# Two products of the first MLP matrix in one 512-column matmul

## The chip, the cores and the metric

One core of a Trainium2 chip runs the whole program. It has a matrix engine (TensorE, PE in the rows, with its weight loads shown apart as PEld), a vector engine (VectorE, DVE), a scalar engine (ScalarE, ACT), GpSimd (POOL) and a sync engine (SP) that issues most of the transfers. The metric is the device time of one execution in microseconds; 1785.32 us is the median of three runs of the kernel before.

## The reference

A hybrid network on 256 tokens of width 1024 in float32: a first block (Fourier and gated delta-rule mixing, a convolutional feed-forward part), then two layers of a second kind. Each of these two layers ends in a plain MLP, which is the part that is changed:

```python
h = rms_norm(x, g_pre_mlp) * (1.0 + sc_f) + sh_f
f = jnp.square(jax.nn.relu(h @ w1)) @ w2
return x + gt_f * rms_norm(f, g_post_mlp)
```

`w1` is 1024 x 4096, `w2` 4096 x 1024; `h` has 256 rows.

## The kernel before

**Split products.** Float32 products are made of three products of a shorter type, `f32r` (`fp32r` in the rows). Each operand is split in a high part (a rounded copy) and a low part (what the copy left), and `mm3` (lines 341 to 344) adds high x high, high x low and low x high in one PSUM region. For a weight tile of 128 x 128 this is three matmuls of 256 columns with the weights `w_hi`, `w_hi`, `w_lo`: line 342 `w_hi` with `act_hi`, line 343 `w_hi` again with `act_lo`, line 344 `w_lo` with `act_hi`. Each matmul has a weight load of its own. In this text the three together are a unit.

**Chunks.** Weights come as chunks of 128 x 2048 values (1 MB, sixteen weight tiles), numbered `n` in the order of use. The sync engine loads chunk `n` in one of four slots `raw` as soon as chunk `n - 4` is done (`chunk_done`). ScalarE copies it to `w_hi` (`prep`, line 1071), VectorE subtracts and writes `w_lo` (`prep`, line 1607). `w_hi` and `w_lo` have two buffers each, so the two copies of chunk `n + 2` can begin only when chunk `n` is done, and have to be ready when chunk `n + 1` is done: `begin` makes TensorE wait for `lo_ready` before a chunk.

**The MLP.** It runs in two halves (`hf` 0 and 1) of 2048 hidden features. Each half has eight chunks of the first product (`feat_chunk`, or `mod_chunk` for the very first, which follows the modulated activations as they come), each 16 units into one bank of PSUM, 0 or 1 in turn, with its two output tiles side by side. Then come eight chunks of the second product (`deep_chunk`), in banks 2 to 5, which use `mlp_hi` and `mlp_lo`, the split of the squared hidden values.

Behind each first-product chunk stands a chain over two engines: ScalarE reads the bank through a ReLU into `relu` (line 1082, signals `evicted`), VectorE squares it into `rsq` (line 2334), ScalarE copies that to `mlp_hi` (line 1572), VectorE writes `mlp_lo` (line 2337). The order on each engine is written out by hand: ScalarE does `prep` of chunk `n + 2` first, then the chain of chunk `n`; VectorE likewise. After the last chunk of a half (`c` = 7) the chain comes first, and then `prep_halves` splits the weights of the second deep chunk, in two pieces of 1024 columns on each engine (lines 1077 and 1078, 1613 and 1615). The first deep chunk needs the last chain only in its last two units; the second deep chunk needs both pieces.

Of the kernel before, what the change touches and what calls it, by code (L numbers as in the profile page):

```python
# [90 lines left out]
def build_program(nc, io, layers=LAYERS):  # L91
# [6 lines left out]
    with ctx:  # L98
# [26 lines left out]
        act_hi = [at(f"act_hi{i}", [P, KT, T], F[i], f32r) for i in range(2)]  # L125
        act_lo = [at(f"act_lo{i}", [P, KT, T], F[2 + i], f32r) for i in range(2)]
# [153 lines left out]

        def JL(o):
            return o if o <= L_LRU else o - 1
# [15 lines left out]
        def _(sp):  # L298
            sp.dma_start(vec[:, :], io["vecs"]).then_inc(S("vec_loaded"), 16)
            sp.dma_start(cc[:, :], io["consts_common"]).then_inc(S("cc_loaded"), 16)  # L300
# [37 lines left out]
        def _(pe):  # L338
# [41 lines left out]
            def mod_chunk(wp, bank, s, m):  # L380

                for k in range(KT):
                    pe.wait_ge(S("mod_lo"), 8 * m + k + 1)
                    for b in range(2):
                        o = (b * KT + k) * P
                        last = mm3(ps[:, bank, b * T:(b + 1) * T], w_hi[:, wp, o:o + P], w_lo[:, wp, o:o + P],
                                   act_hi[s][:, k, :], act_lo[s][:, k, :], k + b == 0, k == KT - 1, shared=True)
                return last
# [106 lines left out]
            pe.wait_ge(S("cc_loaded"), 16)  # L495
# [382 lines left out]
            for L in range(layers):  # L878
# [153 lines left out]
                for hf in range(2):  # L1032
                    n = n0 + L_MLP + 16 * hf
                    j = j0 + JL(L_MLP) + 8 * hf
                    if hf == 0:
                        begin(n, j)
                        mod_chunk(n % 2, j % 2, 1, 4 + 2 * L).then_inc(S("chunk_done"), 1)
                        job(feat_chunk, n + 1, j + 1, 3, 1)
                        job(feat_chunk, n + 4, j + 4, 4, 1)
                    else:  # L1040
                        job(feat_chunk, n, j, 8, 1)
# [14 lines left out]
        def _(act):  # L1056
# [106 lines left out]
            act.wait_ge(S("eps_set"), 1)  # L1163
# [12 lines left out]
            for c in range(2):  # L1176
# [3 lines left out]
                if c == 0:  # L1180
                    act.wait_ge(S("pads"), 3)
# [183 lines left out]
            act.wait_ge(S("gpad_zero"), 1)  # L1365
# [31 lines left out]
            for L in range(layers):  # L1397
                n0, j0 = N_LAYER + L * LAYER_CH, J_LAYER + L * LAYER_J
                ns, sp_ = 5 + 4 * L, 4 * L
                if L == 0:  # L1400
                    act.dma_start(cu[:, 0:N_CB], io["consts_b"]).then_inc(S("consts_b"), 16)
# [161 lines left out]
                for hf in range(2):  # L1563
# [34 lines left out]
        def _(dve):  # L1598
# [115 lines left out]
            nc.vector.memset(eps[:, :], EPS).then_inc(S("eps_set"), 1)  # L1714
# [6 lines left out]
            dve.wait_ge(S("cc_loaded"), 16)  # L1721
# [16 lines left out]
            nc.vector.memset(pre_kv[:, :, :, 0:T + 2:T + 1], 0.0).then_inc(S("pads"), 1)  # L1738
            nc.vector.memset(pre_q[:, :, 0:1], 0.0).then_inc(S("pads"), 1)
            nc.vector.memset(pre_q[:, :, T + 1:T + 2], 0.0).then_inc(S("pads"), 1)  # L1740
# [253 lines left out]
            nc.vector.memset(gpad[:, :, :, :], 0.0).then_inc(S("gpad_zero"), 1)  # L1994
# [91 lines left out]
            for L in range(layers):  # L2086
# [42 lines left out]
                def cum():  # L2129
# [3 lines left out]
                    dve.wait_ge(S("consts_b"), 16)  # L2133
# [192 lines left out]
                for hf in range(2):  # L2326
# [3 lines left out]
                    def mlp_steps(i, c, j=j, hf=hf):  # L2330
                        s = (j + c) % 2
                        e = 8 * (2 * L + hf) + i + c
                        dve.wait_ge(S("evicted"), i + (j + c + 1))
                        tt(rsq[:, s, :], relu[:, s, :], relu[:, s, :], ALU.mult).then_inc(S("mlp_sq"), 1)  # L2334
                        dve.wait_ge(S("mlp_hi"), e + 1)
                        b = bass.ds((i + c) * 2, 2)
                        tt(mlp_lo[:, b, :], rsq[:, s, :].rearrange("p (b t) -> p b t", b=2), mlp_hi[:, b, :].bitcast(f32),
                           ALU.subtract).then_inc(S("mlp_ready"), 1)
                    job(n, 4, hook=mlp_steps)
                    for c in range(4, 7):  # L2340
                        prep(n + c + 2, (n + c + 2) % RAW, (n + c) % 2)
                        mlp_steps(0, c)
                    mlp_steps(0, 7)
# [147 lines left out]
```

## Time and profile before

| what | value |
|---|---|
| median of three runs | 1785.32 us (1782.82 to 1785.48) |
| profiled execution, its span | 1786.7 us, no other time of it is given |
| TensorE matmuls, busy | 1704.3 us, 95% of the span, 15394 |
| TensorE weight loads, busy | 1606.0 us, 90% |
| VectorE, busy | 1097.3 us, 61% |
| ScalarE, busy | 813.0 us, 46% |
| DMA, mean over the span | 184 GB/s |
| mean granted clock of TensorE | 0.988 |

A matmul's length in the rows is the time from its start to the end of its last result; matmuls overlap, so the pace is read from one start to the next. The first products of the MLP run from about 995 to 1041 us and 1087 to 1128 us in the first layer, and from about 1593 to 1639 and 1685 to 1726 us in the second; the second products fill the 40 to 46 us behind each.

### The profile page before, as it was taken

The page shows a single profiled execution, that of the slowest core. Times are in us where ns is not written, and L with a number is a line of the kernel's source. Part 1 is how long each engine was busy: PE and PEld are TensorE (multiplying, and loading weights), DVE is VectorE, ACT ScalarE, POOL GpSimd, SP SyncE. Part 2 cuts the span into 40 slices and gives each one's busy share as a digit, 9 for nine tenths or more (in the row PEclk, how much of TensorE's full clock was granted, in tenths as well). Part 3 has the DMA queues.
Part 4 walks back from the last instruction along what each step waited for, and adds up shares of the span by engine and source line. Part 5 has one row for each costly group of instructions (what it writes and reads, how often), then busy time and mean ns, then how long its engine had stood idle before and what let it go on. Part 6 is the DMA issues. An engine that isn't in the chain of part 4 may idle for free.

```text
span 1786.7 us, 34649 instructions
## 1 busy us (share of the span) xinstructions
PE 1704.3 (95%) x15394; PEld 1606.0 (90%) x15394; DVE 1097.3 (61%) x1367; ACT 813.0 (46%) x1051; POOL 34.2 (2%) x68
## 2 busy tenths in 40 slices
PE   5998899999999899999999999999999999999997
PEld 4896788799988899999999899979999999979997
DVE  3476664679853565468775755555447778666463
ACT  3245414433333535447654444435454575445352
POOL 0000000000000000000000000000000000000000
PEclk8998999999999999999999999999999999999999
DMA  9676433654568444445555355525444445535552
GB/s 397 254 279 235 183 147 128 235 191 167 201 224 328 173 164 162 139 149 178 177 189 182 117 191 196 189 98 186 142 142 165 165 166 189 189 110 185 200 189 71
DMA packets 45210, 329.32 MB, mean 184 GB/s; under 512 B 5008, under 2 KB 5008, under 8 KB 5392
## 3 DMA queue, kind: packets, MB, share of 16 engines
q1 hardware_dynamic: 35712, 258.63, 41.8%
q0 software_dynamic: 9216, 67.11, 9.8%
q8 instruction: 114, 1.87, 0.4%
q10 hardware_dynamic: 144, 1.51, 0.2%
q14 instruction: 24, 0.20, 0.0%
HBM read 326.18 MB, written 1.05 MB: 183 GB/s over the span
## 4 chain that ended last, share of the span: by engine, by line
PE 81%; DVE 9%; ACT 6%; DMA 2%; issue 1%; POOL 0%; SPq 0%; ACTq 0%; DVEq 0%; POOLq 0%
PE ps L342 20%; PE ps L344 20%; PE ps L343 20%; PE ps L395 4%; DVE w_lo L1607 3%; PE ps L467 3%; ACT w_hi L1071 3%; PE ps L446 3%; DMA ada_raw<-ada 2%; PE ps L630 1%; PE ps L641 1%; DVE rstd L1654 1%; DVE x L1692 1%; PE ps L973 1%; DVE rsq L2334 1%
## 5 line engine op out<-in xcount | busy, mean ns | idle before, releaser
L1607 DVE TENSOR_TENSOR w_lo<-raw,w_hi 128x2048 fp32r<-128x2048 f32 x207 | 474.5, 2292 | 489.4 <-ACT w_hi L1071 489.0
L342 PE MATMUL ps<-act_hi,w_hi 128*128 128x256 f32 x2672 | 756.6, 283 | 15.0 <-DVE act_lo L1676 4.6
L343 PE MATMUL ps<-act_lo,w_hi 128*128 128x256 f32 x2672 | 744.9, 279 | 0.0
L344 PE MATMUL ps<-act_hi,w_lo 128*128 128x256 f32 x2672 | 744.8, 279 | 0.0
L1071 ACT ACTIVATE w_hi<-raw 128x2048 fp32r<-128x2048 f32 (+1 forms) x229 | 421.7, 1842 | 551.5 <-PE ps L344 549.0
L342 PEld LDWEIGHTS ps<-act_hi,w_hi 128*128 128x128 f32 x2672 | 504.1, 189 | 25.3 <-issue 16.3
L343 PEld LDWEIGHTS ps<-act_lo,w_hi 128*128 128x128 f32 x2672 | 505.4, 189 | 1.1 <-issue 0.2
L344 PEld LDWEIGHTS ps<-act_hi,w_lo 128*128 128x128 f32 x2672 | 503.6, 188 | 0.0
L342 PE MATMUL ps<-mlp_hi,w_hi 128*128 128x256 f32 x512 | 143.0, 279 | 0.2
L343 PE MATMUL ps<-mlp_lo,w_hi 128*128 128x256 f32 x512 | 141.5, 276 | 0.0
L344 PE MATMUL ps<-mlp_hi,w_lo 128*128 128x256 f32 x512 | 141.5, 276 | 0.0
L342 PEld LDWEIGHTS ps<-mlp_hi,w_hi 128*128 128x128 f32 x512 | 96.1, 188 | 0.8 <-DVE w_lo L1615 0.6
L2031 DVE SCALAR_TENSOR_TENSOR gacc<-gpad,vectors,gacc 128x256 f32<-128x256 f32 x176 | 84.6, 481 | 19.7 <-ACT gacc L1344 14.3
L343 PEld LDWEIGHTS ps<-mlp_lo,w_hi 128*128 128x128 f32 x512 | 96.3, 188 | 0.2
L344 PEld LDWEIGHTS ps<-mlp_hi,w_lo 128*128 128x128 f32 x512 | 96.1, 188 | 0.0
L395 PE MATMUL ps<-h_up,raw 128*128 128x256 f32 x352 | 82.4, 386 | 1.9 <-ACT h_up L1334 1.6
L395 PEld LDWEIGHTS ps<-h_up,raw 128*128 128x128 f32 x352 | 65.4, 192 | 13.5 <-ACT h_up L1334 2.9
L342 PE MATMUL ps<-w_hi,act_hi 128*128 128x256 f32 x256 | 72.2, 282 | 0.0
L467 PE MATMUL ps<-ada_raw,silu_c_wide 128*32 128x256 f32 x1024 | 64.7, 392 | 7.7 <-DMA ada_raw<-ada 7.6
L344 PE MATMUL ps<-w_hi,act_lo 128*128 128x256 f32 x256 | 71.4, 279 | 0.0
L343 PE MATMUL ps<-w_lo,act_hi 128*128 128x256 f32 x256 | 71.3, 278 | 0.0
L467 PEld LDWEIGHTS ps<-ada_raw,silu_c_wide 128*32 128x32 f32 x1024 | 30.2, 111 | 31.5 <-DMA ada_raw<-ada 10.3
(407 smaller groups left out, 2053.3 us busy)
## 6 DMA issues: line engine op xcount, KB each, us to landing
raw<-stream SPq DMA_DIRECT2D x233, 1024.0 KB, 4.9
ada_raw<-ada POOLq DMA_DIRECT2D x64, 1024.0 KB, 7.0
ada_f<-ada SPq DMA_DIRECT2D x4, 1024.0 KB, 14.9
ada_a<-ada SPq DMA_DIRECT2D x3, 1024.0 KB, 20.6
consts_stage<-consts_a SPq DMA_DIRECT2D x1, 1728.0 KB, 32.7
consts_stage<-consts_b ACTq DMA_DIRECT2D x1, 1472.0 KB, 10.6
x<-xT SPq DMA_DIRECT2D x1, 1024.0 KB, 7.9
xc<-ctxT SPq DMA_DIRECT2D x1, 1024.0 KB, 9.9
```

Of the source, the lines that this page charges most:

```text
L342: mm(out, ah, bh, start=first, stop=False, skip_group_check=shared)
L343: mm(out, ah, bl, start=False, stop=False, skip_group_check=shared)
L344: return mm(out, al, bh, start=False, stop=last, skip_group_check=shared)
L395: mm(ps[:, bank, 0:T], raw[:, slot, k * P:(k + 1) * P], h_up[:, k, :], start=k == 0, stop=k == KT - 1)
L446: last = mm(ps[:, 7, 0:T], omean, sq[:, b, :], start=b == 0, stop=b == KT - 1)
L467: last = mm(ps[strip:strip + 32, bank, c * T:(c + 1) * T], cs_wide[:, k, 32 - 3 * j:64 - 3 * j], ada_raw[:, c, k * T:(k + 1) * T], start=j ...
L630: last = mm(ps[r:r + 64, INV_BANK[q], j * 64:(j + 1) * 64], B01[d][r:r + 64, t0 + j // 4, j % 4, r:r + 64], Tm[r:r + 64, q, j, :], start=T ...
L641: last = mm(ps[r:r + 64, INV_BANK[q], j * 32:(j + 1) * 32], Uc[r:r + 64, q, j, :], half(X[r:r + 64, q, j, :], d, 1 << lvl), start=True, st ...
L973: last = mm(out, s1[:, h * 2 + m, t * P:(t + 1) * P], vtok_r[:, m, h * T:(h + 1) * T], start=m == 0, stop=m == t)
L1071: act_(w_hi[:, s2, o:CH], raw[:, s4, o:CH], ACT.Copy).then_inc(S("hi_ready"), 1)
L1607: tt(w_lo[:, s2, :], raw[:, s4, :], w_hi[:, s2, :].bitcast(f32), ALU.subtract).then_inc(S("lo_ready"), 1)
L2031: ins = stt(acc, src, w, acc, ALU.mult, ALU.add)
```

## The change

The activations' high and low parts are put in one tensor, `act_both`, so that `act_hi` and `act_lo` of the same tile can be read by one matmul as 2 x 256 columns. In the first MLP product a unit becomes two matmuls: `w_hi` with 512 columns (high and low activations side by side) into a whole bank, and `w_lo` with `act_hi` added onto the first 256 columns of that bank. A chunk now fills two banks instead of one, (0, 1) or (6, 7) in turn.

The two halves of a bank are added when it is read: ScalarE copies the right halves of both banks to `relu` (signal `side_out`), VectorE adds the left halves (signal `evicted`), and then squares with the ReLU in the same instruction, max with 0 and multiply. On ScalarE the copy of the bank moves ahead of `prep`; on VectorE the add and the square stand ahead of `prep`, and `mlp_lo` behind it. Some semaphores are merged under one name (`cleared`, `consts_loaded`), with counts raised to match; one such line stands in the diff.

```diff
@@ place of the activations @@
-        act_hi = [at(f"act_hi{i}", [P, KT, T], F[i], f32r) for i in range(2)]
-        act_lo = [at(f"act_lo{i}", [P, KT, T], F[2 + i], f32r) for i in range(2)]
+        act_both = at("act_both", [P, 2, 2, KT, T], F[0], f32r)
+        act_hi = [act_both[:, 0, i, :, :] for i in range(2)]
+        act_lo = [act_both[:, 1, i, :, :] for i in range(2)]
...
+        MLP_BANKS = ((0, 1), (6, 7))
...
-            sp.dma_start(cc[:, :], io["consts_common"]).then_inc(S("cc_loaded"), 16)
+            sp.dma_start(cc[:, :], io["consts_common"]).then_inc(S("consts_loaded"), 16)
...
@@ TensorE: new functions @@
+            def wide(banks, wp, s, b, k):
+
+                o = (b * KT + k) * P
+                mm(ps[:, banks[b], :], w_hi[:, wp, o:o + P], act_both[:, :, s, k, :], start=k == 0, stop=False, skip_group_check=True)
+                return mm(ps[:, banks[b], 0:T], w_lo[:, wp, o:o + P], act_hi[s][:, k, :], start=False, stop=k == KT - 1,
+                          skip_group_check=True)
+
+            def wide_chunk(wp, bank, s):
+
+                for b in range(2):
+                    for k in range(KT):
+                        last = wide(MLP_BANKS[bank], wp, s, b, k)
+                return last
+
+            def wide_mod_chunk(wp, bank, s, m):
+
+                for k in range(KT):
+                    pe.wait_ge(S("mod_lo"), 8 * m + k + 1)
+                    for b in range(2):
+                        last = wide(MLP_BANKS[bank], wp, s, b, k)
                 return last
...
@@ TensorE: the MLP @@
-                        mod_chunk(n % 2, j % 2, 1, 4 + 2 * L).then_inc(S("chunk_done"), 1)
-                        job(feat_chunk, n + 1, j + 1, 3, 1)
-                        job(feat_chunk, n + 4, j + 4, 4, 1)
+                        wide_mod_chunk(n % 2, j % 2, 1, 4 + 2 * L).then_inc(S("chunk_done"), 1)
+                        job(wide_chunk, n + 1, j + 1, 3, 1)
+                        job(wide_chunk, n + 4, j + 4, 4, 1)
                     else:
-                        job(feat_chunk, n, j, 8, 1)
+                        job(wide_chunk, n, j, 8, 1)
...
@@ ScalarE: the MLP @@
-                        evict(relu[:, s, :], s, i + (n + c), ACT.Relu)
+                        bank = MLP_BANKS[s][0]
+                        act.wait_ge(S("chunk_done"), n + c + 1)
+                        act_(relu[:, s, :].rearrange("p (b t) -> p b t", b=2), ps[:, bank:bank + 2, T:2 * T], ACT.Copy)\
+                            .then_inc(S("side_out"), 1)
+                        if c < 7:
+                            prep(n + c + 2, (n + c + 2) % RAW, (n + c) % 2)
                         act.wait_ge(S("mlp_sq"), e + 1)
                         act_(mlp_hi[:, bass.ds((i + c) * 2, 2), :], rsq[:, s, :].rearrange("p (b t) -> p b t", b=2), ACT.Copy)\
                             .then_inc(S("mlp_hi"), 1)
-                    job(n, j, 4, None, hook=mlp_steps)
-                    for c in range(4, 7):
-                        prep(n + c + 2, (n + c + 2) % RAW, (n + c) % 2)
+                    for c in range(8):
                         mlp_steps(0, c)
-                    mlp_steps(0, 7)
                     prep_halves(n + 9)
...
@@ VectorE: the MLP @@
-                    def mlp_steps(i, c, j=j, hf=hf):
-                        s = (j + c) % 2
-                        e = 8 * (2 * L + hf) + i + c
-                        dve.wait_ge(S("evicted"), i + (j + c + 1))
-                        tt(rsq[:, s, :], relu[:, s, :], relu[:, s, :], ALU.mult).then_inc(S("mlp_sq"), 1)
-                        dve.wait_ge(S("mlp_hi"), e + 1)
-                        b = bass.ds((i + c) * 2, 2)
+                    def mlp_square(c, n=n, j=j, hf=hf):
+                        s, bank = (j + c) % 2, MLP_BANKS[(j + c) % 2][0]
+                        dve.wait_ge(S("side_out"), 8 * (2 * L + hf) + c + 1)
+                        y = relu[:, s, :].rearrange("p (b t) -> p b t", b=2)
+                        tt(y, ps[:, bank:bank + 2, 0:T], y, ALU.add).then_inc(S("evicted"), 1)
+                        dve.wait_ge(S("evicted"), j + c + 1)
+                        stt(rsq[:, s, :], relu[:, s, :], 0.0, relu[:, s, :], ALU.max, ALU.mult).then_inc(S("mlp_sq"), 1)
+
+                    def mlp_low(c, j=j, hf=hf):
+                        s, b = (j + c) % 2, slice(2 * c, 2 * c + 2)
+                        dve.wait_ge(S("mlp_hi"), 8 * (2 * L + hf) + c + 1)
                         tt(mlp_lo[:, b, :], rsq[:, s, :].rearrange("p (b t) -> p b t", b=2), mlp_hi[:, b, :].bitcast(f32),
                            ALU.subtract).then_inc(S("mlp_ready"), 1)
-                    job(n, 4, hook=mlp_steps)
-                    for c in range(4, 7):
+                    for c in range(7):
+                        mlp_square(c)
                         prep(n + c + 2, (n + c + 2) % RAW, (n + c) % 2)
-                        mlp_steps(0, c)
-                    mlp_steps(0, 7)
+                        mlp_low(c)
+                    mlp_square(7)
+                    mlp_low(7)
                     prep_halves(n + 9, 2 * L + hf + 1)
                     job(n + 8, 8 if hf == 0 else 6)
```

On TensorE, at the end of the first product of a half, where the second product begins. Before, the last unit of the first product and the first of the second:

```order
L342 MATMUL ps<-act_hi_54,w_hi 128x256
L343 MATMUL ps<-act_lo_56,w_hi 128x256
L344 MATMUL ps<-act_hi_54,w_lo 128x256
L342 MATMUL ps<-mlp_hi,w_hi 128x256 [waits lo_ready,mlp_ready]
L343 MATMUL ps<-mlp_lo,w_hi 128x256
L344 MATMUL ps<-mlp_hi,w_lo 128x256
```

Now:

```order
L396 MATMUL ps<-act_both,w_hi 128x512
L397 MATMUL ps<-act_both,w_lo 128x256
L345 MATMUL ps<-mlp_hi,w_hi 128x256 [waits lo_ready,mlp_ready]
L346 MATMUL ps<-mlp_lo,w_hi 128x256
L347 MATMUL ps<-mlp_hi,w_lo 128x256
```

The three matmuls of a unit with their three weight loads have become two; the second product's are as they were.

On ScalarE, the last two chunks of a half (`c` = 6 and 7) and the halves of the second deep chunk's weights. Before:

```order
L1071 ACTIVATE w_hi<-raw 128x2048 [waits chunk_done,raw_loaded0]
L1082 ACTIVATE relu<-ps 128x512 [waits chunk_done]
L1572 ACTIVATE mlp_hi<-rsq 128x512 [waits mlp_sq]
L1082 ACTIVATE relu<-ps 128x512 [waits chunk_done]
L1572 ACTIVATE mlp_hi<-rsq 128x512 [waits mlp_sq]
L1077 ACTIVATE w_hi<-raw 128x1024 [waits chunk_done,raw_loaded1]
L1078 ACTIVATE w_hi<-raw 128x1024
```

Now:

```order
L1597 ACTIVATE relu<-ps 128x512 [waits chunk_done]
L1096 ACTIVATE w_hi<-raw 128x2048 [waits chunk_done,raw_loaded0]
L1602 ACTIVATE mlp_hi<-rsq 128x512 [waits mlp_sq]
L1597 ACTIVATE relu<-ps 128x512 [waits chunk_done]
L1602 ACTIVATE mlp_hi<-rsq 128x512 [waits mlp_sq]
L1102 ACTIVATE w_hi<-raw 128x1024 [waits chunk_done,raw_loaded1]
L1103 ACTIVATE w_hi<-raw 128x1024
```

The copy out of PSUM stands ahead of the weight copy for `c` = 6; for `c` = 7 and the halves the order is the same.

On VectorE, the same place. Before:

```order
L1607 TENSOR_TENSOR w_lo<-raw,w_hi 128x2048 [waits hi_ready]
L2334 TENSOR_TENSOR rsq<-relu 128x512 [waits evicted]
L2337 TENSOR_TENSOR mlp_lo<-rsq,mlp_hi 128x512 [waits mlp_hi]
L2334 TENSOR_TENSOR rsq<-relu 128x512 [waits evicted]
L2337 TENSOR_TENSOR mlp_lo<-rsq,mlp_hi 128x512 [waits mlp_hi]
L1613 TENSOR_TENSOR w_lo<-raw,w_hi 128x1024 [waits half_hi]
L1615 TENSOR_TENSOR w_lo<-raw,w_hi 128x1024 [waits hi_ready]
```

Now:

```order
L2361 TENSOR_TENSOR relu<-ps,relu 128x512 [waits side_out]
L2363 SCALAR_TENSOR_TENSOR rsq<-relu 128x512 [waits evicted]
L1634 TENSOR_TENSOR w_lo<-raw,w_hi 128x2048 [waits hi_ready]
L2368 TENSOR_TENSOR mlp_lo<-rsq,mlp_hi 128x512 [waits mlp_hi]
L2361 TENSOR_TENSOR relu<-ps,relu 128x512 [waits side_out]
L2363 SCALAR_TENSOR_TENSOR rsq<-relu 128x512 [waits evicted]
L2368 TENSOR_TENSOR mlp_lo<-rsq,mlp_hi 128x512 [waits mlp_hi]
L1640 TENSOR_TENSOR w_lo<-raw,w_hi 128x1024 [waits half_hi]
L1642 TENSOR_TENSOR w_lo<-raw,w_hi 128x1024 [waits hi_ready]
```

Each chunk has one instruction more, the add from PSUM; add and square have moved ahead of `w_lo`, and for `c` = 7 the add stands ahead of the square and so of the two pieces of `w_lo`.

## Rows read from the trace of the kernel before

**Rows 1.** The share of the chain that ended last, by engine (page, part 4).
```profile
PE 81%; DVE 9%; ACT 6%; DMA 2%; issue 1%; POOL 0%; SPq 0%; ACTq 0%; DVEq 0%; POOLq 0%
```

**Rows 2.** Busy time by stretch, first half: us, busy by engine in order, PEclk.
```profile
995.00:1041.00 46.00, 45.74 (x385) 45.68 (x386) 29.28 (x33) 23.99 (x27) 0.00 (x0) 1.00 0.47 161
```

**Rows 3.** Timeline, TensorE matmuls, first half of the MLP: start, length, line.
```profile
1009.83 0.28 PE L342 MATMUL ps<-act_hi,w_hi 128*128 128x256 f32 x1
...
1010.18 0.28 PE L342 MATMUL ps<-act_hi,w_hi 128*128 128x256 f32 x1
...
1011.95 0.28 PE L342 MATMUL ps<-act_hi,w_hi 128*128 128x256 f32 x1
```

**Rows 4.** Timeline, TensorE weight loads, the same stretch.
```profile
1010.07 0.19 PEld L342 LDWEIGHTS ps<-act_hi,w_hi 128*128 128x128 f32 x1
```

**Rows 5.** Timeline, TensorE matmuls, second half of the MLP.
```profile
1095.03 0.28 PE L343 MATMUL ps<-act_lo,w_hi 128*128 128x256 f32 x1
...
1097.07 0.28 PE L343 MATMUL ps<-act_lo,w_hi 128*128 128x256 f32 x1
```

**Rows 6.** Groups by shape, TensorE (first row 1095 to 1115 us): count, busy, mean.
```profile
L342 PE MATMUL ps<-act_hi,w_hi 128*128 128x256 f32 x60 | 16.6, 276 | 0.0
...
L973 PE MATMUL ps<-vtok_r,s 128*128 128x256 f32 x48 | 10.7, 379 | 0.0
...
L923 PE MATMUL ps<-s 128*128 128x128 f32 x32 | 6.2, 274 | 0.0
```

**Rows 7.** Timeline, TensorE, sixteen f32 matmuls of 256 columns in a row.
```profile
373.46 3.61 PE L395 MATMUL ps<-h_up,raw 128*128 128x256 f32 x16
```

**Rows 8.** Timeline, TensorE weight loads under matmuls of two columns.
```profile
35.91 1.86 PEld L511 LDWEIGHTS ps<-strip_rows,mod_rows 128*128 128x128 f32 x16 [0.41 <-issue]
```

**Rows 9.** Timeline, ScalarE: one steady chunk, the last chunk of each half.
```profile
1012.92 1.92 ACT L1071 ACTIVATE w_hi<-raw 128x2048 fp32r<-128x2048 f32 x1
1014.74 0.58 ACT L1082 ACTIVATE relu<-ps 128x512 f32<-128x512 f32 x1
...
1041.12 0.60 ACT L1082 ACTIVATE relu<-ps 128x512 f32<-128x512 f32 x1
...
1128.47 0.58 ACT L1082 ACTIVATE relu<-ps 128x512 f32<-128x512 f32 x1
```

**Rows 10.** Timeline, VectorE: one steady chunk, the last chunk of each half.
```profile
1014.87 2.29 DVE L1607 TENSOR_TENSOR w_lo<-raw,w_hi 128x2048 fp32r<-128x2048 f32 x1 [1.37 <-ACT w_hi L1071]
...
1041.76 0.69 DVE L2334 TENSOR_TENSOR rsq<-relu 128x512 f32<-128x512 f32 x1
...
1045.24 1.22 DVE L1615 TENSOR_TENSOR w_lo<-raw,w_hi 128x1024 fp32r<-128x1024 f32 x1
...
1129.21 0.68 DVE L2334 TENSOR_TENSOR rsq<-relu 128x512 f32<-128x512 f32 x1
```

**Rows 11.** Groups by shape, VectorE.
```profile
L1684 DVE TENSOR_TENSOR s<-ps,rstd 128x512 f32<-128x512 f32 x16 | 10.6, 685 | 0.1
...
L2292 DVE SCALAR_TENSOR_TENSOR act_lo<-s,act_hi 128x512 fp32r<-128x512 f32 x8 | 5.3, 686 | 1.7 <-ACT act_hi L1502 1.7
```

**Rows 12.** Timeline, TensorE: second deep chunk of each half; a stage of layer two.
```profile
1046.58 0.33 PE L342 MATMUL ps<-mlp_hi,w_hi 128*128 128x256 f32 x1
...
1133.96 0.38 PE L342 MATMUL ps<-mlp_hi,w_hi 128*128 128x256 f32 x1
1134.18 0.28 PE L343 MATMUL ps<-mlp_lo,w_hi 128*128 128x256 f32 x1
...
1136.22 0.28 PE L343 MATMUL ps<-mlp_lo,w_hi 128*128 128x256 f32 x1
...
1500.99 0.39 PE L342 MATMUL ps<-act_hi,w_hi 128*128 128x256 f32 x1 [0.61 <-DVE w_lo L1607]
1501.22 0.28 PE L343 MATMUL ps<-act_lo,w_hi 128*128 128x256 f32 x1
...
1503.57 0.28 PE L342 MATMUL ps<-act_hi,w_hi 128*128 128x256 f32 x1
```

More of the change, by code:

```diff
@@ L387, in mod_chunk @@
                                    act_hi[s][:, k, :], act_lo[s][:, k, :], k + b == 0, k == KT - 1, shared=True)
+                return last
[8 more added lines that the diff above has]
+                        last = wide(MLP_BANKS[bank], wp, s, b, k)
+                return last
+            def wide_mod_chunk(wp, bank, s, m):
[3 more added lines that the diff above has]
+                        last = wide(MLP_BANKS[bank], wp, s, b, k)
                 return last
@@ L492, in small_tr @@
                 return last
-            pe.wait_ge(S("cc_loaded"), 16)
+            pe.wait_ge(S("consts_loaded"), 16)
             norm(0, norm_sq1)
@@ L1162, in _ @@
             act_(cth[:, :], vec[:, 0:3 * KT], ACT.Tanh, scale=0.5).then_inc(S("c_tanh"), 1)
-            act.wait_ge(S("eps_set"), 1)
+            act.wait_ge(S("cleared"), 1)
             act.wait_ge(S("x_loaded"), 16)
@@ L1180, in _ @@
                 if c == 0:
-                    act.wait_ge(S("pads"), 3)
+                    act.wait_ge(S("cleared"), 4)
                 act_(pre_q[:, 2 * c:2 * c + 2, 1:T + 1], ps[:, n % 2, :].rearrange("p (b t) -> p b t", b=2), ACT.Copy)\
@@ L1364, in up_mid @@
                 act_(mid_hi1[:, bass.ds(i + (c - 2), 1), :], gm[:, c % 2:c % 2 + 1, :], ACT.Copy).then_inc(S("mid_hi"), 1)
-            act.wait_ge(S("gpad_zero"), 1)
+            act.wait_ge(S("cleared"), 5)
             for c in range(4):
@@ L1400, in _ @@
                 if L == 0:
-                    act.dma_start(cu[:, 0:N_CB], io["consts_b"]).then_inc(S("consts_b"), 16)
+                    act.dma_start(cu[:, 0:N_CB], io["consts_b"]).then_inc(S("consts_loaded"), 16)
                 norm_x(ns, x, a6, 5 + 8 * L)
@@ L1711, in softplus @@
                 order(stt(dst, e, 2.0, m, ALU.mult, ALU.add))
-            nc.vector.memset(eps[:, :], EPS).then_inc(S("eps_set"), 1)
+            nc.vector.memset(eps[:, :], EPS).then_inc(S("cleared"), 1)
             dve.wait_ge(S("c_tanh"), 1)
@@ L1720, in _ @@
             order(nc.vector.tensor_copy(cs_wide[:, :, 32:35], cs[:, :, :].rearrange("p a k -> p k a")))
-            dve.wait_ge(S("cc_loaded"), 16)
+            dve.wait_ge(S("consts_loaded"), 16)
             red(sel[:, :], ident.rearrange("p (s r) -> p r s", s=4), AX, ALU.add).then_inc(S("cs_ready"), 1)
@@ L1737, in _ @@
             prep(1, 1, 1)
-            nc.vector.memset(pre_kv[:, :, :, 0:T + 2:T + 1], 0.0).then_inc(S("pads"), 1)
-            nc.vector.memset(pre_q[:, :, 0:1], 0.0).then_inc(S("pads"), 1)
-            nc.vector.memset(pre_q[:, :, T + 1:T + 2], 0.0).then_inc(S("pads"), 1)
+            nc.vector.memset(pre_kv[:, :, :, 0:T + 2:T + 1], 0.0).then_inc(S("cleared"), 1)
+            nc.vector.memset(pre_q[:, :, 0:1], 0.0).then_inc(S("cleared"), 1)
+            nc.vector.memset(pre_q[:, :, T + 1:T + 2], 0.0).then_inc(S("cleared"), 1)
             job(N_Q, 1)
@@ L1993, in _ @@
                  lambda b: tt(act_lo[1][:, b, :], h_up[:, b, :], act_hi[1][:, b, :].bitcast(f32), ALU.subtract))
-            nc.vector.memset(gpad[:, :, :, :], 0.0).then_inc(S("gpad_zero"), 1)
+            nc.vector.memset(gpad[:, :, :, :], 0.0).then_inc(S("cleared"), 1)
             order(nc.vector.memset(sw_wide[:, :, 8:16], 0.0))
@@ L2132, in cum @@
                     dve.wait_ge(S("cum_ev"), L + 1)
-                    dve.wait_ge(S("consts_b"), 16)
+                    dve.wait_ge(S("consts_loaded"), 32)
                 def fox_scores(h0):
```

## The prediction

> **What bounds the kernel now.** I read the share of the last chain first: TensorE carries 81% of it [rows 1]. Then the stretch of the changed stage: in the first half of the MLP TensorE is busy 45.74 of 46 us, VectorE 29.28 and ScalarE 23.99, at a granted clock of 1.00, so the upper of the two levels, 2.4 GHz [rows 2]. The stage is TensorE's, and the question is what paces its matmuls. So, third, the timeline, from start to start: eighteen steps in the first half take 2.12 us, 117.8 ns each [rows 3]; eighteen steps of the same work in the second half 2.04 us, 113.3 ns [rows 5]. The same form thus has two paces, each kept for whole stages at an unchanged clock. The weight loads explain both: a load starts with the matmul before its own (1010.07) and its matmul starts 0.11 us later [rows 3, 4]; and sixteen matmuls of only two columns, where nothing but the load can set the pace, have their loads (1.86 - 0.19) / 15 = 111.3 ns apart [rows 8]. A 256-column matmul is over in the time that the next load needs. Fewer loads for the same columns is a real saving.
>
> **What a unit costs afterwards.** A unit of three matmuls takes 353 ns in the first half and 340 ns in the second. The 512-column `f32r` matmul is not in the trace. Its nearest relative is an `f32` matmul of half the columns: `f32` with 128 columns lasts 274 ns, `f32r` with 256 lasts 276 [rows 6], so `f32r` with 512 should behave as `f32` with 256, which lasts 379 ns [rows 6] and follows itself in (3.61 - 0.38) / 15 = 215.3 ns [rows 7]. That is longer than any load, so the load of `w_lo` hides completely. The 256 columns of `w_lo` then have to cover the load of the next `w_hi`, as now: between 111.3 ns (load alone) and 117.8 ns; I take the middle of the two paces, 115.5. New unit: 331 ns.
>
> First half of a layer: seven chunks of 16 units, 112 x (353 - 331) = 2.5 us. Second half: eight chunks, 128 x (340 - 331) = 1.15 us. The first chunk of a layer, which follows the modulated activations one by one, I count as nothing. Both layers: 7.2 us off. Ends: with 326.6 ns a unit, 9.3 us; with no saving at all (512 columns costing two old paces), 0. A loss I exclude: the columns streamed are the same and a load goes.
>
> **What is added in the middle of a half, and hides.** ScalarE's copy of two half banks has the size of the old ReLU read (0.58 us [rows 9]) but now stands ahead of the weight copy. The chain from a chunk's end to finished weights was w_hi start to w_lo start 1.95 us, then 2.29 us [rows 9, 10]; with 0.58 in front and about 0.06 us for the signal it is 4.9 us, against a new chunk of 16 x 331 = 5.3 us. VectorE's add out of PSUM (685 ns) and the square with max (686 ns for that form) [rows 11] stand ahead of `w_lo`, but run while ScalarE makes `w_hi` (1.92 us), so they cost nothing. Slack 0.4 us; were it gone, each overrun would be paid by TensorE at every chunk. A PSUM bank pair is free after the add, a whole chunk before it is written again. Renamed semaphores and the joined tensor move nothing.
>
> **What is added at the end of a half, and shows.** After the last chunk the chain stands ahead of the two weight pieces of the second deep chunk, on both engines. In the first half it now runs: read 1041.12, square 1041.76 [rows 9, 10], last piece of `w_lo` 1045.24 + 1.22 = 1046.46, and TensorE's second deep chunk starts at 1046.58 [rows 10, 12], a start that TensorE itself would have made at about the same time (its 48 matmuls at 117.8 ns fill 5.65 us). So the cover is just used up, and whatever lengthens the chain is paid in full. The change puts the add ahead of the square: 0.685 us and 0.04 us to the next instruction (the step from the read's end at 1041.72 to the square), 0.725 us. In the second half the square starts only at 1129.21, held by the chunk before; afterwards it would start at 1128.47 + 0.58 + 0.04 + 0.725 = 1129.81 [rows 9, 10], so 0.6 us later. The first deep chunk itself does not wait, since its last two units come some 4.8 us after its start. Per layer 1.33 us, both layers 2.7 us back. Ends: 0.4 us per half (a shorter add) and 1 us.
>
> **The pace after the longer wait.** TensorE keeps whichever of its two paces it falls into after a wait. Behind the 1133.96 start, delayed by the same `w_lo`, it runs eighteen steps in 2.04 us, 113.3 ns; behind a wait of 0.61 us for `w_lo` in layer two it runs twenty steps in 2.35 us, 117.5 ns [rows 12]. Now all four second products start their second chunk after a wait of 0.6 to 1 us. The slow pace would cost 48 x 4.5 ns = 0.216 us a chunk: seven chunks in a first half, and two in a second half, where norm matmuls then break the run: 1.5 and 0.4 us. I take half of the 3.9 us for both layers, 1.9 us, because the rows show one case of each kind. Ends 0 and 3.9.
>
> **Sum.** -7.2 + 2.7 + 1.9 = -2.6 us. Made in the profiled execution it takes its span from 1786.7 to 1784.1 us; the median of the runs lies 1.4 us under that span, so 1785.3 - 2.6 = 1782.7 us.
>
> **A rule against it.** The trace gives 113.3 and 117.8 ns for 256 columns and 215.3 ns for twice the streaming time [rows 3, 5, 7]. The Trainium skill, "TensorE: Matmul & The Clock Gate", section "Back-to-back issue gap", puts a lone warm gap at the columns over 2.4 GHz plus about 2.5 ns, 109.2 and 215.8 ns; the trace agrees with the second and not with the first. An estimate by that page would make a unit 327.5 ns before and 325.0 after, 1.2 us gained in 480 units, and the kernel 3.4 us slower. I go by the rows, which show the load; that the load is not what is saved is rival 2, priced by rows.
>
> **Rivals.**
> 1. The fast pace survives the waits in all four second products. For it: the shorter waits of now all led to it [rows 12]. Against: the wait at 1500.99. -7.2 + 2.7 = -4.5, 1780.8 us.
> 2. The load is not what is saved: the excess belongs to every matmul, so 512 columns cost an old pace plus the lengthening of 105 ns (379 - 274, rows 6), 222.8 or 218.3 ns, and the pair 340.6 or 331.6. Gain 224 x 12.7 + 256 x 8.4 ns = 5.0 us, sum -0.4, 1784.9 us: the change would then remove less than it says. For it: both paces lie above the load's 111.3 ns. Against: sixteen `f32` matmuls show no such excess [rows 7].
> 3. Slower: the second products fall into the slow pace in all 28 chunks behind the waits, norm breaks included. 28 x 0.216 = 6.0 us, sum +1.5, 1786.9 us. It turns the sign from 21 slow chunks on (4.5 / 0.216). For it: the whole first half of now runs slow [rows 3]; against: in the second half of now the fast pace is kept [rows 5].
>
> **Chances.** Forecast 0.50 (own range 1780.5 to 1785), rival 1 0.25, rival 2 0.13, rival 3 0.12. The stages of layer two's mixer start at other moments than now and may change pace too, some 2 us either way, which widens each case. Range 1776.5 to 1787: the low end is the 9.3 us gain with the fast pace (-6.6, 1778.7) and those 2 us, the high end is rival 3. About 3.6 us, 0.2%, is what a measurement of this kernel can tell from no change: faster by more 0.42 (most of rival 1, a third of the forecast, the mixer's part), within 0.50, slower 0.08.
>
> **What would show it.** Right: first products with starts 215 and 113 to 118 ns apart in turn, chunks of about 5.3 us without waits of TensorE for `w_lo`; at each half's end an add of 0.69 us ahead of the square and a wait of 0.6 to 1 us ahead of the second deep chunk. Wrong: a 512-column matmul paced above 225 ns; weight chains longer than a chunk; no wait at the second deep chunk, or one at the first, for `mlp_lo`.

## The result, and the profile after

The changed kernel takes 1793.11 us (median of 18 runs, 1789.45 to 1799.48) against 1784.06 us for the kernel before in the same series (18 runs). The ratio is 1.0048, 95% interval 1.0032 to 1.0064. (It is an estimate from the runs of both kernels and differs a little from the quotient of the two medians, 1.0051.) The changed kernel is slower, outside the range of the prediction, and on the other side from the forecast.

The chain that ended last (page, part 4), by engine, against 81% of TensorE [rows 1]:

```profile
PE 83%; DVE 8%; ACT 5%; DMA 2%; issue 1%; SPq 0%; DVEq 0%; ACTq 0%
```

The first half's stretch, busy time by engine, then granted clock, DMA share and GB/s (after):

```profile
989.00:1035.00 46.00, 45.84 (x258) 39.49 (x259) 34.70 (x41) 23.15 (x27) 0.00 (x0) 1.00 0.45 160
```

As in [rows 2], TensorE is full and at the upper level of its clock. A third of the loads is gone, VectorE has 5.4 us more, and no wait shows: the loss must lie in TensorE's own matmuls. Their starts in the first half and in the second (timeline, TensorE, after):

```profile
1009.74 0.40 PE L396 MATMUL ps<-act_both,w_hi 128*128 128x512 f32 x1
1009.97 0.28 PE L397 MATMUL ps<-act_both,w_lo 128*128 128x256 f32 x1
1010.09 0.40 PE L396 MATMUL ps<-act_both,w_hi 128*128 128x512 f32 x1
...
1012.57 0.40 PE L396 MATMUL ps<-act_both,w_hi 128*128 128x512 f32 x1
...
1096.71 0.40 PE L396 MATMUL ps<-act_both,w_hi 128*128 128x512 f32 x1
1096.94 0.28 PE L397 MATMUL ps<-act_both,w_lo 128*128 128x256 f32 x1
1097.06 0.40 PE L396 MATMUL ps<-act_both,w_hi 128*128 128x512 f32 x1
...
1099.18 0.40 PE L396 MATMUL ps<-act_both,w_hi 128*128 128x512 f32 x1
```

Eight units in 2.83 us and seven in 2.47 us are 353 ns a unit, in steps of 235 and 118 ns. That is three times 117.8, the unit of [rows 3] to the nanosecond: a 512-column matmul costs two 256-column ones at their slow pace, and the load that is gone gives nothing back. In the second half, which ran at 113.3 before [rows 5], the unit has become 13 ns longer.

The chains on ScalarE and VectorE (timeline of each, after; steady chunk, then the last chunk of the first half):

```profile
1006.76 0.60 ACT L1597 ACTIVATE relu<-ps 128x512 f32<-128x512 f32 x1 [2.73 <-PE ps L397]
1007.25 1.91 ACT L1096 ACTIVATE w_hi<-raw 128x2048 fp32r<-128x2048 f32 x1
...
1035.03 0.60 ACT L1597 ACTIVATE relu<-ps 128x512 f32<-128x512 f32 x1 [2.73 <-PE ps L397]
```

```profile
1007.39 0.69 DVE L2361 TENSOR_TENSOR relu<-ps,relu 128x512 f32<-128x512 f32 x1 [0.95 <-ACT relu L1597]
1008.11 0.69 DVE L2363 SCALAR_TENSOR_TENSOR rsq<-relu 128x512 f32<-128x512 f32 x1
1009.19 2.29 DVE L1634 TENSOR_TENSOR w_lo<-raw,w_hi 128x2048 fp32r<-128x2048 f32 x1 [0.39 <-ACT w_hi L1096]
...
1035.66 0.69 DVE L2361 TENSOR_TENSOR relu<-ps,relu 128x512 f32<-128x512 f32 x1 [0.95 <-ACT relu L1597]
1036.38 0.69 DVE L2363 SCALAR_TENSOR_TENSOR rsq<-relu 128x512 f32<-128x512 f32 x1
...
1039.86 1.22 DVE L1642 TENSOR_TENSOR w_lo<-raw,w_hi 128x1024 fp32r<-128x1024 f32 x1
```

In the steady chunk the weights are finished at 1009.19 + 2.29 = 1011.48, 4.7 us after the read of the bank began (4.9 predicted), inside a chunk of 5.65 us; VectorE even waits 0.39 us for `w_hi`. At the half's end the add runs from 1035.66 and the square follows at 1036.38, 0.72 us later than the add began [compare rows 9, 10]. The second deep chunk of each half (timeline, TensorE, after):

```profile
1040.36 0.28 PE L347 MATMUL ps<-mlp_hi,w_lo 128*128 128x256 f32 x1
1041.13 0.39 PE L345 MATMUL ps<-mlp_hi,w_hi 128*128 128x256 f32 x1 [0.49 <-DVE w_lo L1642]
1041.36 0.28 PE L346 MATMUL ps<-mlp_lo,w_hi 128*128 128x256 f32 x1
...
1043.47 0.28 PE L346 MATMUL ps<-mlp_lo,w_hi 128*128 128x256 f32 x1
...
1132.34 0.39 PE L345 MATMUL ps<-mlp_hi,w_hi 128*128 128x256 f32 x1 [0.50 <-DVE w_lo L1642]
1132.57 0.28 PE L346 MATMUL ps<-mlp_lo,w_hi 128*128 128x256 f32 x1
...
1134.62 0.28 PE L346 MATMUL ps<-mlp_lo,w_hi 128*128 128x256 f32 x1
```

TensorE now waits 1041.13 - 1040.36 - 0.12 = 0.65 us, as predicted. Behind the wait of the first half eighteen steps take 2.11 us (117 ns), behind that of the second 2.05 us (114 ns). In [rows 12] both went on at the quick pace.

Stage by stage, from the differences of matmul starts in the traces (from the last of the matmuls that only keep TensorE busy ahead of the MLP to the first deep one, and so on, at last to the first matmul behind the last deep one; both layers alike within 0.02 us):

| us per layer | first product, half 0 | deep, half 0 | first product, half 1 | deep, half 1 | whole MLP |
|---|---|---|---|---|---|
| before | 46.97 | 43.79 | 43.52 | 47.40 | 181.68 |
| after | 46.97 | 45.98 | 45.22 | 48.00 | 186.18 |
| difference | 0.00 | +2.19 | +1.70 | +0.60 | +4.50 |

Two layers make +9.0 us, the size of the difference between the medians. The profiled spans differ by only 0.9 us (1787.6 and 1786.7): in that one execution of the changed kernel the parts ahead of the two MLPs, where the change alters no work, happened to take 6.1 and 2.0 us less. The span of one profile would have passed the change as neutral.

### The profile page after: what moved, and what is told of

It reads as the page before. It is cut to its first block, busy times and chain, and to the rows that moved or that the text cites. A ratio compares the mean times of both kernels' runs of the same rounds, so it can differ in the third digit from the quotient of the medians.

```text
span 1787.6 us, 33657 instructions
## 1 busy us (share of the span) xinstructions
PE 1704.4 (95%) x14882; PEld 1582.5 (89%) x14882; DVE 1119.4 (63%) x1399; ACT 811.3 (45%) x1051; POOL 34.1 (2%) x68
## 4 chain that ended last, share of the span: by engine, by line
PE 83%; DVE 8%; ACT 5%; DMA 2%; issue 1%; SPq 0%; DVEq 0%; ACTq 0%
PE ps L345 18%; PE ps L346 18%; PE ps L347 18%; PE ps L396 7%; PE ps L420 4%; PE ps L397 3%; PE ps L492 3%; PE ps L471 2%; DVE w_lo L1634 2%; DMA raw<-stream 1%; ACT w_hi L1096 1%; PE ps L655 1%; DVE rstd L1681 1%; PE ps L666 1%; DMA ada_raw<-ada 1%
## 5 line engine op out<-in xcount | busy, mean ns | idle before, releaser
L345 PE MATMUL ps<-act_both,w_hi 128*128 128x256 f32 x2160 | 612.4, 284 | 14.9 <-DVE act_both L1703 5.3
L346 PE MATMUL ps<-act_both,w_hi 128*128 128x256 f32 x2160 | 601.8, 279 | 0.0
L347 PE MATMUL ps<-act_both,w_lo 128*128 128x256 f32 x2160 | 601.6, 279 | 0.0
L345 PEld LDWEIGHTS ps<-act_both,w_hi 128*128 128x128 f32 x2160 | 407.6, 189 | 23.6 <-issue 13.9
L346 PEld LDWEIGHTS ps<-act_both,w_hi 128*128 128x128 f32 x2160 | 408.7, 189 | 1.1 <-issue 0.2
L347 PEld LDWEIGHTS ps<-act_both,w_lo 128*128 128x128 f32 x2160 | 407.3, 189 | 0.0
L396 PE MATMUL ps<-act_both,w_hi 128*128 128x512 f32 x512 | 182.0, 399 | 1.4 <-DVE act_both L1698 1.4
L397 PE MATMUL ps<-act_both,w_lo 128*128 128x256 f32 x512 | 143.9, 281 | 0.0
L396 PEld LDWEIGHTS ps<-act_both,w_hi 128*128 128x128 f32 x512 | 96.2, 188 | 27.4 <-issue 3.0
L397 PEld LDWEIGHTS ps<-act_both,w_lo 128*128 128x128 f32 x512 | 96.1, 188 | 0.0
L345 PE MATMUL ps<-w_hi,act_both 128*128 128x256 f32 x256 | 72.1, 282 | 0.0
```

The source lines that it names most:

```text
L345: mm(out, ah, bh, start=first, stop=False, skip_group_check=shared)
L346: mm(out, ah, bl, start=False, stop=False, skip_group_check=shared)
L347: return mm(out, al, bh, start=False, stop=last, skip_group_check=shared)
L396: mm(ps[:, banks[b], :], w_hi[:, wp, o:o + P], act_both[:, :, s, k, :], start=k == 0, stop=False, skip_group_check=True)
L397: return mm(ps[:, banks[b], 0:T], w_lo[:, wp, o:o + P], act_hi[s][:, k, :], start=False, stop=k == KT - 1, skip_group_check=True)
```

## The experiments

The theory formed from these traces: fetching different columns of `f32r` paces these matmuls, at 0.443 or 0.460 ns a column (113.3 and 117.8 over 256), the weight load runs beside it, and a joined matmul saves nothing. The expectations call it theory C, and call the two paces levels: quick (113.3) and slow (117.8). Its rival, from the prediction: loads pace the narrow matmuls, and something in the wide form (two pieces of 256 columns, or a new wait) takes the saving back.

**The wide matmul alone taken back.** Everything of the change stays, the 512 columns are issued as two matmuls.

```diff
-                mm(ps[:, banks[b], :], w_hi[:, wp, o:o + P], act_both[:, :, s, k, :], start=k == 0, stop=False, skip_group_check=True)
+                mm(ps[:, banks[b], 0:T], w_hi[:, wp, o:o + P], act_hi[s][:, k, :], start=k == 0, stop=False, skip_group_check=True)
+                mm(ps[:, banks[b], T:2 * T], w_hi[:, wp, o:o + P], act_lo[s][:, k, :], start=False, stop=False, skip_group_check=True)
```

> The changed kernel with each 512-column matmul split again into two of 256 columns, into the left and right half of the same bank; banks, chain and add stay as changed. Theory C (the pace of an f32r matmul goes by its columns, at 0.443 or 0.460 ns a column, whatever its weight loads; the level is kept until TensorE waits): three starts 118 ns apart where the pair took 235 + 118, a unit again 353 ns, a layer's MLP 186 us, the whole within 2 us of the changed kernel's 1793 us. Theory W (the wide matmul is slow by itself and brings the loss): only the longer chain is left, 1784 + 2.7 = about 1787 us.

1787.08 us, ratio to before 1.0005 (0.9983 to 1.0026). With the same chains, banks and adds, but narrow matmuls, the kernel can't be told from the kernel before. So the joining itself brought the larger part of the loss; the longer chain's 2.7 us lie inside this interval. Theory C, which expected 353 ns here too and about 1793 us, is not borne out: the number of columns alone does not set the time of a unit. The trace (timeline, TensorE):

```profile
1011.87 0.28 PE L397 MATMUL ps<-act_both,w_hi 128*128 128x256 f32 x1
...
1014.13 0.28 PE L396 MATMUL ps<-act_both,w_hi 128*128 128x256 f32 x1
...
1051.39 0.39 PE L345 MATMUL ps<-mlp_hi,w_hi 128*128 128x256 f32 x1 [0.71 <-DVE w_lo L1643]
```

Twenty steps in 2.26 us: 113 ns, in all four first products and, up to the norm matmuls, all four second ones. The stages are 45.41, 44.53, 43.52 and 47.99 us, 181.45 in all. The wait behind the longer chain is there (0.71). Its price in the second half is 47.99 - 47.40 = 0.59 us. In the first half 44.53 - 43.79 = 0.74 us mixes in a pace, since the first deep chunk before still ran at 117.8; against the second trace of the kernel before (below), where it ran at 113.3, the price is 44.53 - 43.91 = 0.62 us.

The profiled execution took 1795.46 us, one of the longest of the twelve, although all these stages ran at the quick pace: the rest of the program varies too.

**A quarter of the load.** The kernel before with 32 of 128 weight columns in the chunks of the first product behind the modulated one.

```diff
...
+                        last = mm3(ps[0:32, bank, b * T:(b + 1) * T], w_hi[:, wp, o:o + 32], w_lo[:, wp, o:o + 32],
+                                   act_hi[s][:, k, :], act_lo[s][:, k, :], k == 0, k == KT - 1)
...
```

> The kernel before, first products with 32 of the 128 weight columns (the other 96 output rows are left out): a quarter of the weight load under the same 256 streamed columns. Theory C: starts stay 113 or 118 ns apart, 15 first-product chunks a layer as long as before. If the load paces 256 columns: starts come down to about 108 ns (half of the 215.3 ns of f32 with 256 columns), 5.2 us a chunk.

Its matmuls, and its loads (timeline of each):

```profile
1011.02 0.28 PE L344 MATMUL ps<-act_hi,w_lo 128*32 128x256 f32 x1
...
1013.29 0.28 PE L343 MATMUL ps<-act_lo,w_hi 128*32 128x256 f32 x1
```

```profile
1011.02 0.11 PEld L342 LDWEIGHTS ps<-act_hi,w_hi 128*32 128x32 f32 x1
```

A load lasts 0.11 us instead of 0.19 [rows 4], and twenty matmuls take 2.27 us, still 113 ns, in all four first products. So the load does not pace them: its being the limit was the prediction's main step, and that falls here. A single run, 1787.82 us.

**The same column over and over, narrow and wide.** Here the loads are whole, but a matmul reads one activation column over and over (the wide one a column of the high part, then one of the low part); first the kernel before, then the changed one.

```diff
...
+                                   act_hi[s][:, k, 0:1].to_broadcast([P, T]), act_lo[s][:, k, 0:1].to_broadcast([P, T]),
...
```

```diff
+                cols = act_both[:, :, s, k, 0:1].to_broadcast([P, 2, T]) if same else act_both[:, :, s, k, :]
+                hi = act_hi[s][:, k, 0:1].to_broadcast([P, T]) if same else act_hi[s][:, k, :]
...
```

> The kernel before, first products (but the first chunk of a layer) with the same single column of the activations read 256 times (step 0), so the products are not the reference's. If fetching 256 different columns of four bytes each sets the 113 and 118 ns: starts come down to 108 ns, half of the 215.3 ns of f32. If the array or the write to PSUM sets it: 113 or 118 ns as before.

> The changed kernel with the same single column of the high and of the low activations read 256 times each (step 0) in the first products, but for the first chunk of a layer, so the products are not the reference's. Theory F (fetching different columns sets the pace above the load's 112 ns; the load saved is real but lies under it): with no columns to fetch the pair shows the saving, 215 + 112 = 327 ns against 3 x 112 = 335 of the same trial with three matmuls. If the wide matmul is slow for another reason: 235 + 112 or more.

Narrow, then wide (timeline, TensorE, of each):

```profile
1002.83 0.28 PE L343 MATMUL ps<-act_lo,w_hi 128*128 128x256 f32 x1
...
1005.06 0.28 PE L342 MATMUL ps<-act_hi,w_hi 128*128 128x256 f32 x1
```

```profile
1014.85 0.38 PE L398 MATMUL ps<-act_both,w_hi 128*128 128x512 f32 x1
1015.07 0.27 PE L399 MATMUL ps<-act_both,w_lo 128*128 128x256 f32 x1
1015.17 0.38 PE L398 MATMUL ps<-act_both,w_hi 128*128 128x512 f32 x1
...
1017.79 0.38 PE L398 MATMUL ps<-act_both,w_hi 128*128 128x512 f32 x1
```

Narrow: twenty steps in 2.23 us, 111.5 ns, neither of the two values expected but that of the loads alone (111.3 [rows 8]). Wide: nine units in 2.94 us, 327 ns, in steps of 218 and 109, as expected. So a saving like the one that the prediction counted exists, 3 x 111.5 - 327 = 7.5 ns a unit where it counted 9 to 22, but only where one column is repeated. This run writes whole banks too, so the width of the result is not what holds the wide form at 235 ns. With real columns a narrow matmul needs 113.3 ns even with the short load above, so the load of 111 ns is already covered. Whether it is the fetching of new columns or their changing values that takes the remainder, these two runs do not tell apart. A single run of each: 1775.92 and 1787.87 us.

**Is it the two pieces?** The 512 columns are read as one contiguous piece of `act_both` (other products than the reference's).

```diff
+                cols = act_both[:, 0, s, min(k, 6):min(k, 6) + 2, :] if one else act_both[:, :, s, k, :]
+                mm(ps[:, banks[b], :], w_hi[:, wp, o:o + P], cols, start=k == 0, stop=False, skip_group_check=True)
...
```

> The changed kernel with the 512 columns read as one piece (high parts of two neighbouring tiles, so the right halves hold other sums than the reference's), not as two pieces 16 KB apart; the first chunk of a layer as changed. If the two pieces hold the wide matmul at its slow level: pairs of 227 + 113 = 340 ns. If not: 235 + 118 = 353 ns again.

235 and 118 ns as before, first products 46.96 and 45.22 us: not the two pieces. A single run, 1792.27 us.

**Only 512-column matmuls.** The second matmul of a unit gets 512 columns too.

```diff
-                return mm(ps[:, banks[b], 0:T], w_lo[:, wp, o:o + P], act_hi[s][:, k, :], start=False, stop=k == KT - 1,
+                return mm(ps[:, banks[b], :], w_lo[:, wp, o:o + P], act_both[:, :, s, k, :], start=False, stop=k == KT - 1,
...
```

> The changed kernel with 512 columns for w_lo too (low weights times low activations is added to the sum, which makes it a little more exact). Theory C: time goes by columns, so a pair costs 471 ns at 0.460 ns a column or 453 at 0.443, and a first-product chunk 7.5 or 7.25 us. If only a matmul of 512 columns followed by one of 256 is held at the slow level: 453. If a 512-column matmul had the 215 ns of two f32 passes and the 20 ns were a price of the pair: 431.

Steps of 233 ns in the first half, and in the second of 236 ns (`w_lo`) and 230 to 231 ns (`w_hi`) in turn, 467 ns a pair in both: 0.45 to 0.46 ns a column, not the 0.42 (215.3 / 512) that the prediction assumed. So a 512-column matmul is not slow only for having a narrow one behind it. A single run, 1853.36 us.

**The wide form with a quarter of the load.**

```diff
+                mm(ps[0:32, banks[b], :], w_hi[:, wp, o:o + 32], act_both[:, :, s, k, :], start=k == 0, stop=False, skip_group_check=True)
+                return mm(ps[0:32, banks[b], 0:T], w_lo[:, wp, o:o + 32], act_hi[s][:, k, :], start=False, stop=k == KT - 1,
...
```

> The changed kernel with 32 of 128 weight columns in the first products (96 output rows left out): loads of 108 instead of 188 ns under 512 and 256 columns. If the full load that falls into a 512-column stream holds it at the slow level: 340 ns a pair. If the level has nothing to do with loads, as 113 ns with thin loads for 256 columns suggests: 353 ns.

The narrow step stays at 118 ns, so the slow pace does not need the long load either; the wide one is 224 in some places and 232 to 233 in others, 228 on average, against 235, so a unit takes 347 ns, neither of the two values expected. In this one trace the load thus has a small part in the wide form's slow pace, and not the whole. A single run, 1790.08 us. Why the wide form falls to the slow pace is not settled by this.

**The wait at the second deep chunk taken away, without and with the change.** The two weight pieces are split around the copy to `mlp_hi` (and `mlp_lo`): the first now stands ahead of it, the second behind.

```diff
+            def prep_halves(n, between):
...
                 act_(w_hi[:, n % 2, 0:CH // 2], raw[:, n % RAW, 0:CH // 2], ACT.Copy).then_inc(S("half_hi"), 1)
+                between()
                 act_(w_hi[:, n % 2, CH // 2:CH], raw[:, n % RAW, CH // 2:CH], ACT.Copy).then_inc(S("hi_ready"), 1)
...
```

> The kernel before, with the first half of the second deep chunk's weights made ahead of mlp_hi and mlp_lo of the last chunk, on both engines, so that TensorE has no wait at the second deep chunk. If the level is kept until TensorE waits (theory C): the second products and the next first products stay at the slow 117.8 ns of the first half, deep products of the first half 45.3 instead of 43.8 us, first products of the second half 45.2 instead of 43.5 us, the waits of 0.04 and 0.4 us gone: some 2.8 us a layer, 1784 + 5.6 = about 1790 us, although a wait was removed. If waits only cost what they last: 1784 - 0.9 = about 1783 us.

> The changed kernel with the same reordering at the end of a half. Theory C: the waits of 0.65 and 0.7 us ahead of the second deep chunks go, the slow level stays, as it has been slow already: 2 x 1.3 us less, 1793 - 2.6 = about 1790.5 us, a layer's MLP 184.9 us; with the second half's deep products slow as well up to the first norm, 0.4 us of it a layer is lost. If the slow level of the second products came from the wait: they turn fast, 1793 - 2.6 - 6.4 = about 1784 us.

The kernel before so edited: 1783.67 us, 0.9974 (0.9955 to 0.9993); the changed one: 1795.3 us, 1.0049 (1.0030 to 1.0068), no better than without the edit, though the 2.6 us expected are too few to be told within this interval. The waits are gone from both traces. But in both, the MLP stays at the slow pace (235 and 118 ns, 118 ns) from its start to the norm matmuls among the last deep chunks (185.50 and 185.09 us for layer one): with no wait between, the pace did not change. The first of these traces is of the longest of its thirteen executions, 1800.16 us, so its slow MLP does not explain the median of 1783.67 us.

**Both kernels again, and the edit again.** To see what of a trace belongs to the kernel and what to the execution.

> The kernel before, unchanged, in another execution. If the level of a stage is drawn anew in each execution: first products of the first half at 340 or 353 ns a unit, not the same in every execution, though alike in both layers of one. If code and data fix it: slow first half, fast second half, as in the first trace.

> The changed kernel, unchanged, in another execution. Theory: the pair of 512 and 256 columns falls to the slow level wherever it starts: all four first products at 353 ns a unit again; the second products behind the waits may be fast or slow. If wide pairs draw their level as 256-column matmuls do: some first product at 340.

> The kernel before with the reordered end of a half, once more, since its trace was of its slowest execution, with all stages of the MLP at the slow level, while its median was 0.26% under the kernel before. If levels are drawn anew and kept until TensorE waits: now often fast from the first chunk on through the second half up to the norms, a layer's MLP 180.5 us, the median again 0.1 to 0.4% under the kernel before; the waits removed alone are 0.9 us, 0.05%. If the first timing was chance: ratio 1.000 within 0.002.

Before: 1784.61 us, 0.9998 (0.9980 to 1.0016). Changed: 1792.61 us, 1.0037 (1.0019 to 1.0054), so the loss is confirmed. The edit: 1790.61 us, 1.0021 (1.0000 to 1.0043), so its gain is not; its runs go from 1775.89 to 1795.66. The same stretch of the kernel before without the wait, in its two traces (timeline, TensorE, first trace, then second):

```profile
1019.79 0.28 PE L344 MATMUL ps<-act_hi,w_lo 128*128 128x256 f32 x1
...
1022.14 0.28 PE L343 MATMUL ps<-act_lo,w_hi 128*128 128x256 f32 x1
```

```profile
1019.91 0.28 PE L343 MATMUL ps<-act_lo,w_hi 128*128 128x256 f32 x1
...
1022.17 0.28 PE L342 MATMUL ps<-act_hi,w_hi 128*128 128x256 f32 x1
```

Twenty steps take 2.35 us (117.5 ns) in one and 2.26 us (113 ns) in the other, and so on up to the norm matmuls: an MLP of 185.50 us against 179.48 in layer one, 11.6 us over two layers, with no difference in the program. The spans, 1798.4 and 1778.3 us, differ by more, so other parts vary as well.

The kernel before had its first half at 118 in the first trace and at 113 in the second (46.97 and 45.42 us); behind the wait of the second half its deep chunks ran at 113 and then, up to the norm matmuls, at 118. The changed kernel had all four first products at 235 and 118 in both traces, as had the contiguous form and the changed kernel without waits: sixteen stages of sixteen, from four executions. The second products behind its waits were at 118 in half 0 and 113 in half 1; in the second trace at 113 in layer one and at 118 in layer two (up to the norm matmuls). The second pair of traces gives the change +9.5 us over both MLPs, close to the +9.0 of the first pair, but with +6.5 us in the first products, because the kernel before ran both halves quickly this time.

The same trace of the changed kernel shows that the slow wide form is no accident of a wait. In layer one the second products before the second half ran at 113 ns, and TensorE goes on without a wait (timeline, TensorE, changed kernel, second trace):

```profile
1081.46 0.28 PE L347 MATMUL ps<-mlp_hi,w_lo 128*128 128x256 f32 x1
1081.58 0.28 PE L345 MATMUL ps<-mlp_hi,w_hi 128*128 128x256 f32 x1
1081.69 0.28 PE L346 MATMUL ps<-mlp_lo,w_hi 128*128 128x256 f32 x1
1081.80 0.28 PE L347 MATMUL ps<-mlp_hi,w_lo 128*128 128x256 f32 x1
1081.92 0.39 PE L396 MATMUL ps<-act_both,w_hi 128*128 128x512 f32 x1
1082.14 0.28 PE L397 MATMUL ps<-act_both,w_lo 128*128 128x256 f32 x1
1082.26 0.40 PE L396 MATMUL ps<-act_both,w_hi 128*128 128x512 f32 x1
1082.49 0.28 PE L397 MATMUL ps<-act_both,w_lo 128*128 128x256 f32 x1
1082.61 0.40 PE L396 MATMUL ps<-act_both,w_hi 128*128 128x512 f32 x1
...
1083.67 0.40 PE L396 MATMUL ps<-act_both,w_hi 128*128 128x512 f32 x1
```

The first wide matmul takes 0.22 us, from the next on a unit takes 353 ns, and the narrow matmuls of the first deep chunk behind this half keep 118 ns until the wait. The contiguous form shows the same. So a change of form can change the pace too, not only a wait.

## Why the prediction was wrong

**The step that failed is "The weight loads explain both" (in "What bounds the kernel now"), and with it "What a unit costs afterwards": 331 ns a unit predicted, 353 measured.** The reasoning went from two numbers that were near each other: a pace of 113.3 to 117.8 ns for the matmul, 111.3 ns for the load alone. The prediction took the second as the cause of the first. The quarter load, still at 113 ns, shows that they are two separate limits, 2 ns apart at the quick pace. The second error was that the 512-column `f32r` matmul was given the pace of an `f32` one of 256 columns, because the lengths of their halves agreed (276 and 274 ns). Even the length came out at 399 ns against 379, and the step from start to start at 235 ns against 215.3. The length of a matmul did not tell its pace.

The terms, both layers, in us, from the first pair of traces:

| term | predicted | measured | how |
|---|---|---|---|
| first products | -7.2 | +3.4 | 2 x (0.00 + 1.70); +6.5 in the second pair |
| longer chain at a half's end | +2.7 | +2.6 | 2 x (0.68 + 0.60), the 0.68 being 2.19 less the pace |
| pace behind the wait | +1.9 | +3.0 | 2 x 336 steps x 4.5 ns, half 0 |
| sum | -2.6 | +9.0 | |

**A loss was excluded, wrongly.** "The columns streamed are the same and a load goes" bounds the work, but not the pace: the wide form fell to the slow one in every trace with real columns and whole loads, and the narrow form could be at either. By estimate, the 480 units of both layers at 353 instead of 340 ns are 6.2 us, near the 5.7 to 7.7 us by which the changed kernel stands above the split one (ratios 1.0037 and 1.0048 against 1.0005). The split kernel's trace had the quick pace in every first product.

**Rival 2** had the right half, that the load is not what is saved, and still gave the pair 331.6 to 340.6 ns; 353 was beyond all the cases. The estimate by the Trainium skill, "TensorE: Matmul & The Clock Gate", section "Back-to-back issue gap", 3.4 us slower, had the sign, but from the other two terms: it too let the joined unit gain 2.5 ns. The 109.2 and 215.8 ns that the prediction takes from it, for a lone gap, are neared among the `f32r` runs only with one column repeated (109 and 218), while real columns took 113.3 to 117.8 and 235.

**What held.** In the middle of a half the copy, the add and the square are hidden, with more room than predicted because the chunk did not become shorter. The end of a half costs nearly what the chain said: 0.725 and 0.6 us predicted, 0.68 and 0.60 in the changed kernel, 0.62 and 0.59 in the split one. The pace behind the wait differed from trace to trace, as assumed; the slow pace behind all four waits, rival 3, came out behind two of four in each of the two traces. A slow chunk costs the 48 x 4.5 = 0.216 us that rival 3 counted.

**Open.** Why the wide form keeps to the slow pace, and what decides between the paces of the narrow one, is not shown. The trials with short loads, repeated columns, one piece and two wide matmuls are one run and one trace each, and the two layers of one trace are no independent cases. No version here is shown to beat the kernel before; taking the wait away gave 0.9974 once and 1.0021 once.

## What to carry to other kernels

When a pace in the trace lies within 2% of a suspected limit, halve the limit by itself in one run before counting its removal as a gain: here the quarter load would have told it beforehand. Read the pace of an operation that is not in the trace from one that reads as many columns of its own type, not from one whose length happens to agree. And compare timed series, not two profiles: here the spans of two profiles differed by 0.9 us where the medians differed by 9 us, and a stage's pace in one execution need not be the kernel's.

## What the runs showed of the hardware

- `f32r` matmuls with weight loads ran at one of two paces at a granted clock of 1.00, 113.3 and 117.8 ns for 256 columns, kept through whole stages. Narrow stages without a wait of TensorE between them kept it for both halves (at 118 in one trace of the kernel before without the wait, at 113 in the other); behind a wait it could change, and behind the first wide matmuls it changed from 113 to 118 without one. The two MLPs of one execution mostly agreed, two executions of one kernel need not.
- 512 columns took 235 ns beside a 256-column matmul in sixteen stages of sixteen (four executions), 230 to 236 among their like, 224 to 233 with a quarter of the load, and 218 where one column was repeated. A quarter of the load left a 256-column matmul at 113.3 ns. Repeating one column took it to 111.5 ns with a load each, and to 109 with a load less.
- Between two executions of one program, the kernel before without the wait, the two paces alone moved the two MLPs by 11.6 us (185.50 and 179.48 us in layer one), more than the 9.0 us of the change.
